# A two-layer diffusion trunk: the norm on VectorE and ScalarE with two chunks in turn, inverse roots on six token-major columns

## What is computed

```python
def rms_norm(x, g=None):
    y = x * rsqrt(mean(x * x, axis=-1) + 1e-6)
    return y * g if g is not None else y

for l in range(2):
    h = modulate(rms_norm(x, g_mix[l]), shift, scale)      # the same for the context tokens
    # three mixers on h: retention (y = rms_norm(y) * silu(g)), latent attention
    # (q and kv through rms_norm of 256-wide ranks), grouped attention (q and k normed per head)
    x = x + gate * (gated_sum(branches) @ w_out)
    h2 = modulate(rms_norm(x, g_ffn[l]), shift2, scale2)
    x = x + gate2 * ((silu(h2 @ a) * (h2 @ b)) @ w_ffn_out)
return rms_norm(x, g_final)
```

## Time and profile before

| | |
|---|---|
| median of 3 runs | 3745.88 us (3745.24 to 3748.95) |
| the profiled execution | 3743.77 us, its span 3741.9 us |
| granted TensorE clock, mean | 0.938 of full |
| TensorE busy | 3305.7 us, 88% of the span |
| VectorE | 1550.6 us, 41% |
| ScalarE | 1281.4 us, 34% |
| POOL | 477.3 us, 13% |

### The profile page before, as it was taken

The page is one execution under the profiler, slowest core; times in us unless marked ns, Lnnn a source line. Parts: engine busy times, 40 slices in busy tenths (PEclk is TensorE's granted clock), DMA queues, the critical chain, the costliest instruction groups (busy, mean ns, idle before and its releaser), DMA issues.

```text
span 3741.9 us, 50235 instructions
## 1 busy us (share of the span) xinstructions
PE 3305.7 (88%) x18696; PEld 2786.6 (74%) x18696; DVE 1550.6 (41%) x1997; ACT 1281.4 (34%) x1778; POOL 477.3 (13%) x340
## 2 busy tenths in 40 slices
PE   6788897999999988799999967988798999879998
PEld 4678776888888876588888746777677777758886
DVE  4455423544334433422222245653455344453334
ACT  3344332444333332221211223443344333433222
POOL 2011100111000000300000130220011001021001
PEclk8888898999999999899999978999899999989999
DMA  4111141111321123124233231212111321223332
GB/s 159 55 43 56 38 124 40 61 56 60 115 65 62 53 91 128 51 63 133 73 95 107 96 124 54 68 59 84 56 58 61 99 64 62 82 93 100 93 99 95
DMA packets 91434, 297.11 MB, mean 79 GB/s; under 512 B 10320, under 2 KB 16592, under 8 KB 91344
## 3 DMA queue, kind: packets, MB, share of 16 engines
q1 hardware_dynamic: 55872, 202.40, 17.1%
q10 hardware_dynamic: 35472, 93.49, 7.6%
HBM read 274.88 MB, written 20.97 MB: 79 GB/s over the span
## 4 chain that ended last, share of the span: by engine, by line
PE 40%; issue 9%; DVE 6%; ACT 3%; DMA 3%; POOL 1%; ACTq 0%; DVEq 0%; POOLq 0%
PE ps L1278 37%; DMA mraw<-in_wmod 2%; DVE prob L1001 1%; PE ps L1366 1%; DVE mx L838 1%; PE ps L1344 1%; POOL ptl L1260 1%; ACT pth L437 1%; DVE tmp L983 0%; DVE tmp L817 0%; ACT wh L384 0%; DVE wl L807 0%; DVE ptl L856 0%; DVE xz L1165 0%; DVE tmp L877 0%
## 5 line engine op out<-in xcount | busy, mean ns | idle before, releaser
L1278 PE MATMUL ps<-hh,wh 128*128 128x512 f32 x2768 | 835.0, 362 | 123.0 <-POOL hl L1242 64.0
L1278 PE MATMUL ps<-hl,wh 128*128 128x512 f32 x2768 | 823.1, 358 | 0.0
L1278 PE MATMUL ps<-hh,wl 128*128 128x512 f32 x2768 | 820.5, 357 | 0.0
L807 DVE TENSOR_TENSOR wl<-raw,wh 128x1024 fp32r<-128x1024 f32 x364 | 481.9, 1324 | 696.8 <-ACT wh L384 669.3
L1278 PEld LDWEIGHTS ps<-hh,wh 128*128 128x128 f32 x2768 | 457.7, 192 | 223.9 <-issue 59.0
L1278 PEld LDWEIGHTS ps<-hh,wl 128*128 128x128 f32 x2768 | 458.5, 192 | 78.5
L1278 PEld LDWEIGHTS ps<-hl,wh 128*128 128x128 f32 x2768 | 459.9, 193 | 73.6
L384 ACT ACTIVATE wh<-raw 128x1024 fp32r<-128x1024 f32 x364 | 382.8, 1052 | 245.9 <-PE ps L1278 202.6
L1278 PE MATMUL ps<-yh,wh 128*128 128x512 f32 (+1 forms) x1296 | 410.2, 371 | 37.4 <-DVE yl L1132 17.1
L1278 PE MATMUL ps<-yl,wh 128*128 128x512 f32 (+1 forms) x1296 | 397.8, 361 | 0.0
L1278 PE MATMUL ps<-yh,wl 128*128 128x512 f32 (+1 forms) x1296 | 397.4, 361 | 0.0
(11 more groups left out here) (176 smaller groups left out, 3729.3 us busy)
## 6 DMA issues: line engine op xcount, KB each, us to landing
raw<-in_stream SPq DMA_DIRECT2D x364, 512.0 KB, 3.6
mraw<-in_wmod ACTq DMA_DIRECT2D x80, 512.0 KB, 3.7
gspill<-prob ACTq DMA_DIRECT2D x24, 384.0 KB, 2.3
tmp<-gspill ACTq DMA_DIRECT2D x24, 384.0 KB, 3.1
early<-in_wmod SPq DMA_DIRECT2D x16, 512.0 KB, 15.0
dec<-in_dec ACTq DMA_DIRECT2D x8, 768.0 KB, 4.2
gspill<-side ACTq DMA_DIRECT2D x24, 256.0 KB, 2.2
tmp<-gspill ACTq DMA_DIRECT2D x24, 256.0 KB, 2.7
```

Of the source, the lines that this page charges most:

```text
L807: dve.tensor_tensor(wl[:, s, :], raw[:, s, :], wh[:, s, :].bitcast(F32), ALU.subtract).then_inc(sem("w_lo"), 1)
L1278: ins = pe.matmul(out, lhs[w], rhs[x](cols), start=start and n == 0, stop=stop and n == 2)
```

## The change

- **Norm.** VectorE writes `tmp` = `xz` x gain x scales in one instruction per piece, ScalarE writes `hh` = `tmp` + shift, VectorE writes `hl` = (`tmp` + shift) - `hh`. POOL and `prob` are left out. The scales are read from `AUX` in PSUM, but for the first norm.
- **Two chunks in turn.** `project_pair` projects the first two chunks tile by tile together, in mla_in and in the first turn of ffn, which is taken out of its loop. Their second `split` moves ahead of the root.
- **Inverse roots on columns.** The squares are now the stationary operand and one column of ones the moving one: the sum for 128 tokens lands on 128 partitions in one column, so 768 tokens are 6 columns (`sums`). Root and reciprocal work on 128 x 6 (`rt`). `diagonal` multiplies the identity by each column, and `spread`, a product with ones, brings the values back to all partitions, in `AUX`. Only the first norm's squares keep the old way. A one-column root (`warm`) stands ahead of each wait for the sums.
- **Places.** In mla_in and gqa_in `halved` projects a chunk in two halves with the ones product or the sums between them; in ret the ones product of a turn stands in the middle of chunk 0 of the next turn, whose first turn is taken out of the loop, and the last one's behind the loop.

```diff
+            def root(at, n, dst, src):
+                if at.v("chunk") < NCHUNK:
+                    split(at, 1)
+                act.activation(warm[:, :], eps[:, :], ACT.Sqrt)
                 act.wait_ge(sem("sq_used"), at.v("sq_used", n))
-                act.activation(tmp[:, 2, 0:nt], pair(AUX)[:, 0:nt], ACT.Sqrt, bias=eps[:, :],
-                               scale=1.0 / D).then_inc(sem("n_std"), 1)
+                act.activation(dst, src, ACT.Sqrt, bias=eps[:, :], scale=1.0 / D).then_inc(sem("n_std"), 1)
...
                             ins = act.activation(hh[:, t, r0:r1], tmp[:, t % 2, r0:r1], ACT.Identity,
-                                                 bias=mods[:, layer, 3 * gi * KT + t, u:u + 1],
-                                                 scale=gm[:, gi, t, u:u + 1])
+                                                 bias=mods[:, layer, 3 * gi * KT + t, u:u + 1])
...
+            def diagonal(dst, nt):
+                nq = nt // P
+                return dve.tensor_tensor(dst[:, 0:nt].rearrange("p (j q) -> p j q", q=P),
+                                         ident[:, :].unsqueeze(1).to_broadcast([P, nq, P]),
+                                         rt[:, 0:nq].unsqueeze(2).to_broadcast([P, nq, P]), ALU.mult)
+
+            def rstd(at, k, nt, dst):
                 dve.wait_ge(sem("v_std"), at.v("v_std", k + 1))
-                dve.reciprocal(tmp[:, 2, 0:nt], tmp[:, 2, 0:nt]).then_inc(sem("v_rstd"), 1)
+                dve.reciprocal(rt[:, 0:nt // P], rt[:, 0:nt // P]).then_inc(sem("v_rstd"), 1)
                 dve.wait_ge(sem("v_rstd"), at.v("v_rstd", k + 1))
+                diagonal(dst, nt).then_inc(sem("v_diag"), 1)
...
-                            dve.tensor_tensor(tmp[:, t % 2, 0:nt], xz[:, t, 0:nt], tmp[:, 2, 0:nt],
-                                              ALU.mult).then_inc(sem("n_t1"), 1)
+                            for u, (r0, r1) in enumerate(ranges(nt)):
+                                ins = dve.scalar_tensor_tensor(out=tmp[:, t % 2, r0:r1], in0=xz[:, t, r0:r1],
+                                                               scalar=gm[:, gi, t, u:u + 1], in1=scales[:, r0:r1],
+                                                               op0=ALU.mult, op1=ALU.mult)
+                            ins.then_inc(sem("n_t1"), 1)
                         m = t - 1
                         if m >= 0:
+                            dve.wait_ge(sem("n_hi"), at.v("n_hi", m + 1))
                             for u, (r0, r1) in enumerate(ranges(nt)):
-                                ins = dve.tensor_scalar(prob[:, m % 2, r0:r1], tmp[:, m % 2, r0:r1],
-                                                        gm[:, gi, m, u:u + 1],
-                                                        mods[:, layer, 3 * gi * KT + m, u:u + 1], ALU.mult, ALU.add)
+                                ins = dve.scalar_tensor_tensor(
+                                    out=hl[:, m, r0:r1], in0=tmp[:, m % 2, r0:r1],
+                                    scalar=mods[:, layer, 3 * gi * KT + m, u:u + 1],
+                                    in1=hh[:, m, r0:r1].bitcast(F32), op0=ALU.add, op1=ALU.subtract)
+                            ins.then_inc(sem("n_lo"), 1)
...
-                        pool.tensor_tensor(hl[:, t, 0:nt], prob[:, t % 2, 0:nt], hh[:, t, 0:nt].bitcast(F32),
-                                           ALU.subtract).then_inc(sem("n_lo"), 1)
...
+            def project_pair(at, nt):
+                for slot in range(2):
+                    if at.v(f"free{slot}") > 0:
+                        pe.wait_ge(sem(f"free{slot}"), at.v(f"free{slot}"))
+                pe.wait_ge(sem("w_lo"), at.v("chunk", 2))
+                for kt in range(KT):
+                    pe.wait_ge(sem("n_lo"), at.v("n_lo", kt + 1 - KT))
+                    for slot in range(2):
+                        ins = three(...)
+                        if kt == KT - 1:
+                            ins.then_inc(sem("product"), 1)
+
+            def sums(srcs, nt):
+                for j in range(nt // P):
+                    for n, x in enumerate(srcs):
+                        ins = pe.matmul(pair(AUX)[:, j:j + 1], x[:, j * P:(j + 1) * P], ones[:, 0:1], ...)
+            def spread(diag, nt):
+                for r0, r1 in ranges(nt):
+                    ins = pe.matmul(pair(AUX)[:, r0:r1], ones[:, :], diag[:, r0:r1], start=True, stop=True)
...
                 elif kind == "mla_in":
+                    project_pair(at, first)
+                    for j, nt_j in enumerate((first, TOK)):
+                        if j:
+                            halved(at, 2, 0, 1, TOK, lambda: ranked(0, first))
+                            project(at, 3, 1, 1, H, KT, TOK, whole)
...
+                        sums([prob[:, 0, :], prob[:, 1, :]], nt_j).then_inc(sem("v_stat"), 1)
                     project(at, 4, 0, 2, H, KT // 2, TOK, whole, ktn=KT, piece=True)
+                    ranked(1, TOK)
                     project(at, 5, 0, None, H, KT // 2, TOK, whole, kt0=KT // 2, ktn=KT, piece=True)
...
+                        halved(at, 2 * j + 1, 1, j, TOK, key_sums)
+                        pe.wait_ge(sem("v_diag"), at.v("v_diag", j + 1))
+                        spread(tmp[:, 2, :], TOK).then_inc(sem("v_bc"), 1)
                         pe.wait_ge(sem("free1"), at.v("free1", j + 1))
...
+                        halved(t, 0, 0, 0, TOK, (lambda: None) if first else (lambda: normed(t)))
```

More of the change, by code:

```diff
@@ L577, in _ @@
                         act.activation(tmp[:, t % 2, 0:nt], xz[:, t, 0:nt], ACT.Square).then_inc(sem("sq"), 1)
-                    root(at, KT, nt)
+                    root(at, KT, tmp[:, 2, 0:nt], pair(AUX)[:, 0:nt])
                 elif kind == "summed":
-                    root(at, 1, nt)
+                    root(at, 1, rt[:, 0:nt // P], pair(AUX)[:, 0:nt // P])
                 elif kind == "norm":
@@ L735, in turn @@
                             split(t, 7)
[L736 to L738 removed]
+                        std(t, 0, nt, RET_DV)
                         for e in range(2):
@@ L781, in _, with turn @@
                 elif kind == "ffn":
-                    with act.Fori(0, turns) as i:
+                    def turn(i, paired=False):
                         t = At(ph, i)
                         for k in range(2):
-                            split(t, 2 * k + 1)
+                            if not paired or k:
+                                split(t, 2 * k + 1)
                             act.wait_ge(sem("product"), t.v("chunk", 2 * k + 1))
@@ L792, in _ @@
                                            ACT.Copy).then_inc(sem("f_hi"), 1)
+                    if ph["paired"]:
+                        turn(0, paired=True)
+                    with act.Fori(1 if ph["paired"] else 0, turns) as i:
+                        turn(i)
                 elif kind == "final":
@@ L987, in _ @@
                     gi = 0 if ph["first"] else 1
+                    scales = pair(AUX) if layer or not ph["first"] else tmp[:, 2, :]
                     for t in range(KT + 1):
@@ L1180, in _, with turn @@
                 elif kind == "ffn":
-                    with dve.Fori(0, turns) as i:
+                    def turn(i, paired=False):
                         t = At(ph, i)
                         for k in range(2):
-                            split(t, 2 * k + 1)
+                            if not paired or k:
+                                split(t, 2 * k + 1)
                             split(t, 2 * k + 2)
@@ L1190, in _ @@
                                               ALU.mult).then_inc(sem("free1"), 1)
+                    if ph["paired"]:
+                        turn(0, paired=True)
+                    with dve.Fori(1 if ph["paired"] else 0, turns) as i:
+                        turn(i)
                 elif kind == "final":
@@ L1595, in _ @@
                         pe.wait_ge(sem("y_sq"), t.v("y_sq", 2))
-                        for r0, r1 in ranges(nt):
-                            for e, x in enumerate((tmp[:, 0, r0:r1], prob[:, 2, r0:r1])):
-                                ins = pe.matmul(pair(AUX)[:, r0:r1], ones[:, :], x, start=e == 0, stop=e == 1)
-                        ins.then_inc(sem("v_stat"), 1)
+                        sums([tmp[:, 0, :], prob[:, 2, :]], nt).then_inc(sem("v_stat"), 1)
+                    turn(0, first=True)
+                    with pe.Fori(1, turns) as i:
+                        turn(i)
+                    normed(At(ph, end=True))
                 elif kind == "out":
```

140 lines of the change are left out of this document (80 added, 60 removed).

## The result

The changed kernel takes **3719.9 us** (median of 7 runs, 3711.0 to 3726.0). The kernel before, run in turn with it, takes 3745.9. The ratio is 0.9928, with a 95% interval of 0.9914 to 0.9943. The profiled execution has a span of 3718.1 us (before 3741.9) and a mean granted clock of 0.941 (before 0.938). A second set of six runs, beside other kernels, gives 3719.9 and 0.993 (0.9913 to 0.9947).

The account below looks back on a forecast made before the run. TensorE bounds plain projection; in the norm stages products wait for POOL's `hl`. Gains 14.4 + 11.0 + 15.0 + 5.9 + 0.5 less 5, 2 and 5.2 give 34.6 us: 3743.8 to 3709.2, median 3711, range 3698 to 3729.

Parts of the forecast that it names:

- The norm loop: Norm stages: without POOL, VectorE sets a period of 2.4 us a tile instead of 3.35, and TensorE's clock comes back.
- The first stage: Layer 0, first norm with its paired projection: ends at 68.3 instead of 82.7 us, a gain of 14.4.
- The second: Norm before the first feed-forward block: 16.3 us gained, less an uncovered pause before chunk 2 and low clock, net +11.0.
- The third: Third norm: first `hh` waits for ScalarE's eight spills; end at 2227.2 instead of 2242.2 us, a gain of 15.0.
- The fourth: Fourth norm, 512 columns: 10.9 us gained, less 3.0 of lost cover and 2 of low clock, net +5.9.
- The low-rank inputs: Sums gain nothing (2.7 against 2.82 us), ScalarE empties both chunks first: a loss of 2 in layer 0, 3 in layer 1.
- Retention: Ones products inside chunk 0 and longer sums cost 8 us, the last turns gain 1.8 and 1.0: sum -5.2.
- The keys: Grouped attention: diagonal, ones product and sums replace the 4.8 us reciprocal; a loss of 1 us a layer, -2 in all.
- (d): Rival: norm stages speed up, but low-rank and key places lose 8 us more than counted; 3719 to 3722, 14%.
- (b): Rival: TensorE's new waits for the diagonal each drop its clock, 8 exposed places x 2 us more; 3727, 10%.
- (a): Rival: the clock stays low or falls again in the paired norm loop; 3742, 5%; half of it 3727, 9%.
- (c): Rival: the diagonal costs as much as the reciprocal in 14 exposed chains, 4 us each; 3767, 4%.

Follow-up runs that it names:

- Experiment 11: The kernel of experiment 8 with the low-rank inputs' roots put back on one-column sums, ones products and halved chunk: 3705.7 us, ratio 0.9897.
- experiment 6: The changed kernel with every column sum (norm scales, low-rank inputs, keys, retention) moving 128 columns of ones instead of one: 3693.7 us, ratio 0.9857.
- experiment 3: The changed kernel with only retention's inverse root back on wide sums, root and reciprocal, without a ones product in chunk 0: 3708.3 us, ratio 0.9907.
- experiment 4: The changed kernel with only retention's column sums moving 128 columns of ones instead of one: 3704.4 us, ratio 0.9896.
- experiment 10: New norm loop and pairing, wide sums everywhere, plus unread column sums in each retention turn: 3726.3 us with one column, 3706.9 with 128.
- experiment 8: New norm loop and pairing, wide roots in low-rank inputs and retention, 128-column sums for norm scales and keys: 3690.5 us, ratio 0.9852.

## Why the prediction was right, and where it wasn't

**The norm loop: right, and a little better.** The period is 2.24 us, forecast 2.4. The first stage gives 14.8 (82.7 to 67.9), forecast 14.4. The second gives 13.6 from the start of the sums to chunk 2 (46.0 before, 1538.33 to 1584.3; 32.4 now, 1535.05 to 1567.48), less 1.7 for the low clock behind the pause: 11.9, forecast 11.0. The third gives 17.2 from the sums to the end of chunk 1 (45.8 before, 2196.43 to 2242.26; 28.6 now, to 2213.7, where the second product ends), forecast 15.0; its rows:

```profile
2185.07 2.72 PE L1354 MATMUL ps<-ones,prob 128*128 128x1 f32 x12 [2.80 <-POOL prob L1273]
...
2187.84 6.93 ACTq L592 DMA_DIRECT2D xspill<-xz  x8
...
2213.02 0.60 ACT L614 ACTIVATE tmp<-ps 128x512 f32<-128x512 f32 x1 [2.35 <-PE ps L1309]
```

The fourth gives 8.6 by the ledger (296 to 360), forecast 5.9. From VectorE's start to the product behind the pause it takes 18.0 us, where the stage before took 25.7:

```profile
3333.02 1.41 DVE L1021 SCALAR_TENSOR_TENSOR tmp<-xz,gm,ps 128x512 f32<-128x512 f32 x2 [2.17 <-PE ps L1361]
...
3350.99 0.47 PE L1309 MATMUL ps<-hh,wh 128*128 128x512 f32 x1 [2.30 <-DVE wl L816]
```

With 0.5 at the end these are 53.0 us, 6 more than the 46.8 of the sum. The terms were a little too careful one by one: the period; the pauses, 2.2 and 2.3 us where I counted 3.3, since I took both products to end at once and the first ends up to 1.0 us ahead; and the 2 us of low clock behind each pause. They came behind the second stage (1.7) and not behind the fourth, where the products from 3351.30 on take 0.39 us each, as at the full clock.

**The low-rank inputs: the term that failed first.** I counted -2 and -3. It was -6.6 in each layer (48.0 us against 41.4, and 42.6 against 36.0 from 2213.7 to 2256.3). The mechanism that I named is there, and smaller: ScalarE empties both chunks one behind the other, but starts at the end of the first, so the sums begin 3.0 us after the products (forecast 4.3), and the last wait shrinks to 5.1. The size of "24 products, 2.7 us, nothing gained" was wrong. I took it from 12 products in 1.47 us and left it at the full clock. 24 in a row took 5.25 and 3.93 us, and the products behind them ran at the low level as well. The very row that I took the price from is followed by a fall, in the kernel before:

```profile
815.50:818.90 3.40, 3.40 (x12) 2.81 (x12) 1.37 (x4) 3.19 (x4) 1.47 (x1) 0.50 0.00 0
```

Three of the eight query norms of layer 0 have such a stretch behind their sums there (from 631, 692 and 815). Experiment 11 shows that this part costs some 12 to 15 us against wide sums, and experiment 6 that with 128 columns the loss is 4, what was forecast.

**Retention: the term that failed most.** I counted -8 in the loops and +2.8 in the last turns. With 128 columns, where only the work is left, a turn of layer 0 is 0.9 to 1.4 us longer and the two layers come to +0.5 and +3.1 in the ledger. So the work was no more than forecast, and that nothing would stall behind the diagonal was right too. What I didn't count is the clock: 2.6 us a turn. Experiments 3, 4, 6 and 10 show it, by taking it away three times and by adding it once.

**The keys** came out near nothing (-0.4 and +1.4 in two profiles of layer 0, -0.3 and -1.2 in layer 1, splits 222 to 230; forecast a loss of 1 a layer). The groups of the ones products show the new waits for the diagonal, of all places together:

```profile
L1361 PE MATMUL ps<-tmp,ones 128*128 128x512 f32 x24 | 19.4, 902 | 18.0 <-DVE tmp L827 18.0
L1361 PE MATMUL ps<-prob,ones 128*128 128x512 f32 x16 | 10.3, 728 | 2.9 <-DVE prob L827 2.9
```

They are 20.9 us in ten waits (the longest 3.8), in the place of waits for the reciprocal.

**The rivals.** The time is that of (d), "it does less than it says: the low-rank and key places lose 8 us more", 3719 to 3722. Half of it is what happened: the low-rank places lost 8 us more, the keys 2 to 3 less, and retention lost 10 to 15 more, which was in no rival. The norm stages' 6 us on the other side made up for much of that. So it is luck that the time falls on (d)'s number, and that the forecast is only 9 us off. The measured terms, 53.0 - 13.2 + 0.7 - 15.7, give 24.8 us; the two profiled spans differ by 23.8. (b), the clock falls at the new waits, named the right quantity and, for most of it, the wrong cause. The falls that cost are behind the sums, in experiment 10 also with no diagonal in the chain. Behind one wait for the diagonal there is a fall, of 3.4 us at 575, but the kernel before has one as long at 594. I had read the granted clock only in the norm loop, where I feared it, and took the earlier trace rows for the price of a column sum anywhere. (a) and (c) fell.

**The two rules.** VectorE's two pairs for a tile take 1.15 us each, and a tile takes 2.24 us in all. By the prediction's estimate from the Trainium skill (VectorE: DVE Perf Modes, "The perf-mode tier table") this loop would have cost some 28 us; it gained. The table's order is in the trace all the same, where GpSimd is idle: a `tensor_scalar` of 128x512 takes 0.54 us there (3349.60 in the kernel before) and a plain product 0.69 (3350.25), though not half. Beside GpSimd at work the old pair took 2.37 us, and that is what the new loop got rid of. ScalarE's table load ahead of the root takes 1.28 us, from 1534.00, and the next instruction starts at 1535.30, so the drain that the Trainium skill adds (ScalarE: Activation LUTs, "What ACT_TABLE_LOAD costs") isn't seen here.

**What is open.** Why the low level lasts 6.9 us in the first norm loop of the changed kernel (46.0 to 52.9) and 13.7 in that of experiment 6 (42.4 to 56.1), with the same code there, wasn't settled. It moves a stage by 2 to 4 us and is likely a good part of the spread between runs. Between one and 128 moved columns nothing was tried, and no run has the sums of retention without the wait ahead of them (1.60 us in layer 0). For the scales of the norms the number of columns isn't settled: in the second norm the clock is low for 17.1 us in the change and in experiment 8 (128 columns), and twice for 3.4 us in experiment 6 (128 columns).

## What to carry to other kernels

Split a change into the parts that its diff mixes, and time them apart. Here a faster loop worth 45 us hid a statistic that cost 15 to 22, and the whole looked like a modest success. Read TensorE's granted clock over every new run of products, not only where you fear for it: here runs of 24 one-column sums let it fall, and the products behind them paid. The row that a price is taken from is worth reading on: the fall stood right behind it. If a matmul with one moving column takes as long as one with 128, try 128; it cost next to nothing here and was worth 26 us.

## What was unexpected of the hardware

- Products of fp32 with one moving column and with 128 both start every 0.11 us (24 in 2.7 us) at the full clock. With the first the granted clock falls to 0.50 while TensorE is busy: 0.62 in the 9 us from the sums on, against 1.00 with the same wait of 1.60 us ahead. I had expected waits alone to decide it.
- The 12 sums of the keys, in the midst of full projection products and with no wait ahead (565.71), took 1.40 us and left the clock up.
- A product of two operands that are both broadcast views (identity by blocks, six roots by columns) takes VectorE 0.96 us for 128x768, no more than a plain one. The reciprocal of the same size takes 4.95.
- GpSimd issued seven of the eight spills in 3.91 us, where ScalarE took 6.69 for eight. The eighth came 6.8 us later, which nobody waited for.
